# First blocks right behind their own group's turns, modulation weights in four slots, level products one slot later, four loads per chunk in the attention sweep

## What is computed

```python
mod = c_act @ w_mod[l] + b_mod[l]
shift, scale, gate = jnp.split(mod[:, None, :], 3, axis=-1)
h = rms_norm(x, g_pre[l]) * (1.0 + scale) + shift
(gq, gk, gv, ga_f, ga_b, gz, cq, ckv, kr, mz) = _split(h @ w_in_e[e], EVEN_SPLITS)

def step(state, inp):                      # GLA, one direction, one chunk
    qc, kc, vc, gc = inp
    b = jnp.cumsum(gc, axis=2)
    diff = b[:, :, :, None, :] - b[:, :, None, :, :]
    decay = jnp.exp(jnp.where(mask[None, None, :, :, None], diff, -jnp.inf))
    att = jnp.einsum('bhid,bhjd,bhijd->bhij', qc, kc, decay)
    o = jnp.einsum('bhij,bhjv->bhiv', att, vc) + jnp.einsum('bhid,bhdv->bhiv', qc * jnp.exp(b), state)
    b_last = b[:, :, -1, :]
    state = jnp.exp(b_last)[..., None] * state + jnp.einsum(
        'bhjd,bhjv->bhdv', kc * jnp.exp(b_last[:, :, None, :] - b), vc)
    return state, o
o = rms_norm((o_f + o_b).astype(z.dtype), g_norm).reshape(B, S, GLA_WIDTH)
return o * jax.nn.silu(z)
```

## Time and profile before

| | us |
|---|---|
| median of three runs | 3487.02 |
| lowest and highest | 3482.92, 3491.3 |
| profiled execution, its own time | 3487.6 |
| its span on the core | 3485.7 |
| PE busy (share of the span) | 3094.9 (89%) |
| DVE busy | 1376.7 (39%) |
| ACT busy | 1145.9 (33%) |
| POOL busy | 641.5 (18%) |

### The profile page before, as it was taken

The page is one execution under the profiler, slowest core; times in us unless marked ns, Lnnn a source line. Parts: engine busy times, 40 slices in busy tenths (PEclk is TensorE's granted clock), DMA queues, the critical chain, the costliest instruction groups (busy, mean ns, idle before and its releaser), DMA issues.

```text
span 3485.7 us, 47947 instructions
## 1 busy us (share of the span) xinstructions
PE 3094.9 (89%) x17396; PEld 2611.6 (75%) x17396; DVE 1376.7 (39%) x2428; ACT 1145.9 (33%) x2055; POOL 641.5 (18%) x565
## 2 busy tenths in 40 slices
PE   1788999755588999999899499999999999999999
PEld 1556888645577888888788388877888888877887
DVE  4356677511155767676532511112222222222111
ACT  1462245311224555555422611113333223323110
POOL 1021121034231212122122000002112112213221
PEclk6898999866679999999999799999999999999999
DMA  6132355463322111121155211112122122124322
GB/s 206 46 105 97 98 153 161 135 180 104 87 59 74 56 47 54 49 58 51 56 175 181 112 73 72 48 65 78 54 72 72 59 68 72 66 84 152 109 96 72
DMA packets 272009, 318.45 MB, mean 91 GB/s; under 512 B 26323, under 2 KB 206803, under 8 KB 268404
## 3 DMA queue, kind: packets, MB, share of 16 engines
q1 hardware_dynamic: 271894, 316.90, 28.1%
HBM read 214.07 MB, written 102.76 MB: 91 GB/s over the span
## 4 chain that ended last, share of the span: by engine, by line
PE 79%; issue 5%; DVE 4%; POOL 3%; DMA 3%; ACT 3%; SPq 1%; POOLq 0%; DVEq 0%; ACTq 0%
PE PS L325 11%; PE PS L326 10%; PE PS L327 10%; PE PS L2090 4%; PE PS L2091 4%; PE PS L2092 4%; PE PS L2195 3%; PE PS L2197 3%; PE PS L2196 3%; PE PS L1551 3%; PE PS L1573 2%; PE PS L1574 2%; PE PS L1575 2%; PE PS L1540 2%; PE PS L2333 2%
## 5 line engine op out<-in xcount | busy, mean ns | idle before, releaser
L325 PE MATMUL PS<-hTh,whi 128*128 128x512 f32 x1664 | 658.0, 395 | 7.5 <-POOL wlo L319 7.5
L326 PE MATMUL PS<-hTl,whi 128*128 128x512 f32 x1664 | 650.1, 391 | 0.0
L327 PE MATMUL PS<-hTh,wlo 128*128 128x512 f32 x1664 | 649.7, 390 | 0.0
L325 PEld LDWEIGHTS PS<-hTh,whi 128*128 128x128 f32 x1664 | 313.9, 189 | 80.6 <-issue 10.5
L327 PEld LDWEIGHTS PS<-hTh,wlo 128*128 128x128 f32 x1664 | 313.7, 189 | 66.2
L326 PEld LDWEIGHTS PS<-hTl,whi 128*128 128x128 f32 x1664 | 313.9, 189 | 62.8
L317 POOL TENSOR_TENSOR whi<-wraw,zero 128x1024 fp32r<-128x1024 f32 x52 | 99.9, 1922 | 1029.5 <-PE PS L327 975.5
L2090 PE MATMUL PS<-ow_h,of_h 128*128 128x512 f32 x576 | 225.0, 391 | 7.7 <-DVE oy L2047 7.7
L2091 PE MATMUL PS<-ow_l,of_h 128*128 128x512 f32 x576 | 224.8, 390 | 0.0
L2092 PE MATMUL PS<-ow_h,of_l 128*128 128x512 f32 x576 | 224.7, 390 | 0.0
L1649 ACT ACTIVATE pth<-PS 128x512 fp32r<-128x512 f32 x256 | 153.6, 600 | 188.9 <-PE PS L1551 188.9
(11 more groups left out here) (251 smaller groups left out, 6024.3 us busy)
## 6 DMA issues: line engine op xcount, KB each, us to landing
projT<-pev SPq DMA_DIRECT2D x80, 256.0 KB, 2.5
xt<-x SPq DMA_DIRECT2D x8, 2048.0 KB, 8.8
mw<-wmod SPq DMA_DIRECT2D x64, 256.0 KB, 2.8
oxt<-x SPq DMA_DIRECT2D x32, 512.0 KB, 4.8
sg_v<-vev SPq DMA_DIRECT2D x64, 256.0 KB, 2.3
wraw<-wuz SPq DMA_DIRECT2D x32, 512.0 KB, 5.7
vm<-sg_v SPq DMA_DIRECT2D x16, 1024.0 KB, 5.6
sgT<-mT SPq DMA_DIRECT2D x16, 1024.0 KB, 4.4
```

The source lines that it names most:

```text
L325: pe.matmul(PS[:, bank, :], w[1][:, s, k, :], hTh[:, k, b], start=(k == 0), stop=False)
L326: pe.matmul(PS[:, bank, :], w[1][:, s, k, :], hTl[:, k, b], start=False, stop=False)
L327: mm = pe.matmul(PS[:, bank, :], w[2][:, s, k, :], hTh[:, k, b], start=False, stop=(k == KD - 1))
```

## The change

- **Modulation weights.** `mw0` has four slots; load n waits for sum n-4. The first eight tiles are those of the first half of the columns (shift), the next eight those of the second (scale), and PE makes the columns of a half when its eight sums are done. x of group 1 is loaded right behind the last modulation weights, and the first projection weights wait for all sums, since the slots now lie over `wraw0`.
- **First blocks.** Block 0 stands right behind turns 6 and 7; six turns of the next group follow block 0, 2 and 4, two follow blocks 1, 3 and 5. ACT's list follows.
- **Levels.** Each slot y now holds distances and exponential for y, products for y-1, PE's level products for y-1 and sums for y-2; loads run three units ahead. k and q have semaphores of their own, so that distances don't wait for them. The attention matrix is written to memory in the layout in which the sweep reads it, by two instructions of 64 partitions in place of one of 128, on DVE and on ACT.
- **The sweep.** Four loads a chunk (decays; k and q; values and states, now one tensor `gla_vs`; attention) and one for the gate input z, which has its own semaphore and is waited for only by the gate product. Load t+4 stands ahead of store t-2 in SP's list and waits for outputs t. Factors are made one round ahead. Contribution and outputs use other PSUM banks.

The diff, cut:

```diff
-        mw0 = at("mw0", X0 + 8 * K, [P, 2, D])
+        mw0 = at("mw0", X0 + 8 * K, [P, 4, D])
...
-        def mod_load(sp, k):
-            for j in range(2):
-                n = 2 * k + j
-                if n >= 2:
-                    sp.wait_ge(s_macc, n - 1)
-                sp.dma_start(mw0[:, j, :], a["wmod"][0, k * P:(k + 1) * P, j * D:(j + 1) * D]).then_inc(s_mw[j], 16)
+        def mod_load(sp, n):
+            half, k = n // KD, n % KD
+            if n >= 4:
+                sp.wait_ge(s_macc, n - 3)
+            sp.dma_start(mw0[:, n % 4, :], a["wmod"][0, k * P:(k + 1) * P, half * D:(half + 1) * D]).then_inc(s_mw[n % 4], 16)
...
-            mod_cols(pe, macc0, 0).then_inc(s_mps, 1)
+            for half in range(2):
+                pe.wait_ge(s_macc, KD * (half + 1))
+                mm = mod_cols(pe, macc0, half)
+            mm.then_inc(s_mps, 1)
...
-            for k in range(KD):
-                mod_load(sp, k)
+            for n in range(2 * KD):
+                mod_load(sp, n)
+            norm_load(sp, 0, (1,))
+            sp.wait_ge(s_macc, 2 * KD)
             for g in range(2):
                 proj_load(sp, g)
-            norm_load(sp, 0, (1, 2))
+            norm_load(sp, 0, (2,))
             for g in range(2, 4):
...
-                for half in range(2):
-                    for k in range(4):
-                        norm_act(act, 8 * g + 4 * half + k)
-                    proj_evict(act, 2 * g - 2 + half)
+                proj_evict(act, 2 * g - 2)
+                for k in range(6):
+                    norm_act(act, 8 * g + k)
+                proj_evict(act, 2 * g - 1)
+                for k in range(6, 8):
...
-            for m in range(6, 14):
+            for m in range(6, 8):
                 norm_pe(pe, m)
             for j in range(8):
                 proj_block(pe, j)
-                for m in range(12 + 4 * j if j else 14, min(16 + 4 * j, 32)):
-                    norm_pe(pe, m)
+                g = j // 2 + 1
+                if g < 4:
+                    for k in (range(6, 8) if j % 2 else range(6)):
+                        norm_pe(pe, 8 * g + k)
 
...
-            dve.wait_ge(s_ll[s], 48 * (t // 2 + 1))
+            dve.wait_ge(s_ll[s], 32 * (t // 2 + 1))
...
+            dve.wait_ge(s_lk[t % 2 * 2 + p], 16 * (t // 2 + 1))
...
-            dve.tensor_tensor(l_att[:, p, :, 0, :], x[:, :, 0:HB], x[:, :, 2 * HB:3 * HB], ALU.add).then_inc(s_ma, 1)
+            for b in range(2):
+                mine = slice(HB * b, HB * b + HB)
+                dve.tensor_tensor(l_att[mine, p, :, mine], x[mine, :, 0:HB], x[mine, :, 2 * HB:3 * HB], ALU.add).then_inc(s_ma, 1)
...
-            level_exp(act, 0)
             for y in range(NU):
                 j, n = 16 + 2 * y, y - Y_BACK
                 proj_evict(act, j)
-                if y + 1 < NU:
-                    level_exp(act, y + 1)
+                level_exp(act, y)
                 if n >= 0:
...
-            level_distances(dve, 0)
             for y in range(NU):
                 n = y - Y_BACK
                 if n >= 1:
                     back_state(dve, n - 1)
-                if y + 1 < NU:
-                    level_distances(dve, y + 1)
-                level_products(dve, y)
+                level_distances(dve, y)
+                if y:
+                    level_products(dve, y - 1)
                 if n >= 0:
                     back_turned(dve, n)
-                if y:
-                    level_sums(dve, y - 1)
+                if y >= 2:
+                    level_sums(dve, y - 2)
                 if n == -2:
...
-                level_pe(pe, y)
+                if y:
+                    level_pe(pe, y - 1)
+            level_pe(pe, NU - 1)
...
+                sp.dma_start(m_fe[:, s].rearrange("p d h c -> p (d h) c"), cumT[0:4, :, tok].rearrange("n p c -> p n c")
+                             ).then_inc(s_ml[s], 16)
+                sp.dma_start(m_kq[:, s].rearrange("p h w c -> p (h w) c"), projT[T_GK:T_GK + 4, :, tok].rearrange("n p c -> p n c")
+                             ).then_inc(s_ml[s], 16)
+                sp.dma_start(m_vs[:, s, :], gla_vs[t, :, :]).then_inc(s_ml[s], 16)
+                sp.wait_ge(s_las[0], 16 * (t + 1))
+                sp.wait_ge(s_las[1], 16 * (t + 1))
+                sp.dma_start(attT[:, s, :, :], gla_a[t, :, :, :]).then_inc(s_ml[s], 16)
+
+            def load_z(t):
+                if t >= 4:
                     sp.wait_ge(s_mgz, t - 3)
-                for dst, src in ((m_f, cumT[0:2, :, tok]), (m_e, cumT[2:4, :, tok])):
-                    sp.dma_start(dst[:, s, :, :], src.rearrange("h p c -> p h c")).then_inc(s_ml[s], 16)
-                for w, r in ((0, T_GQ), (1, T_GK)):
-                    sp.dma_start(m_qk[:, s, w, :, :], projT[r:r + 4:2, :, tok].rearrange("h p c -> p h c")).then_inc(s_ml[s], 16)
-                sp.dma_start(m_v[:, s, :], gla_v[t, :, :]).then_inc(s_ml[s], 16)
-                sp.dma_start(attT[0:HB, s, :, :].rearrange("p h c -> p (h c)"),
-                             gla_a[t, 0:HB, :, :, :].rearrange("p h d c -> p (h d c)")).then_inc(s_ml[s], 16)
-                for d in range(2):
-                    sp.dma_start(attT[HB:P, s, :, HB * (1 - d):HB * (2 - d)], gla_a[t, HB:P, :, d, :]).then_inc(s_ml[s], 16)
-                sp.dma_start(m_s[:, s, :, :].rearrange("p h v -> p (h v)"), gla_sb[t, :, :]).then_inc(s_ml[s], 16)
-                sp.dma_start(m_z[:, s, :, :], projT[T_GZ:T_GZ + 4, :, tok].rearrange("h p c -> p h c")).then_inc(s_ml[s], 16)
+                sp.dma_start(m_z[:, t % 4, :, :], projT[T_GZ:T_GZ + 4, :, t * P:(t + 1) * P].rearrange("h p c -> p h c")
+                             ).then_inc(s_mzl[t % 4], 16)
 
             def store(t):
                 sp.wait_ge(s_mgz, t + 1)
                 sp.dma_start(mixT[0:GH, :, t * P:(t + 1) * P].rearrange("h p c -> p h c"), og[:, t % 2, :, :]
                              ).then_inc(s_mst[t % 2], 16)
             sp.wait_ge(s_pb, 8 + NBLK)
-            for j in (NBLK - 2, NBLK - 1):
-                stored(sp, j)
             sp.wait_ge(s_bvs, 16 * NT)
             for u in range(2):
                 sp.wait_ge(s_bss[u], 8 * NT)
-                sp.wait_ge(s_las[u], 16 * NT)
             for t in range(4):
                 load(t)
+            for j in (NBLK - 2, NBLK - 1):
+                stored(sp, j)
+            for t in range(4):
+                load_z(t)
+            for u in range(2):
+                sp.wait_ge(s_las[u], 16 * NT)
             rot_sp(sp)
             latents_sp(sp)
-            for t in range(NT):
-                store(t)
+            for t in range(NT + 2):
                 if t + 4 < NT:
                     load(t + 4)
+                if t >= 2:
+                    store(t - 2)
+                    if t + 2 < NT:
+                        load_z(t + 2)
...
             factors(0)
-            factors(1)
...
-                if t + 2 < NT:
-                    factors(t + 2)
+                if t + 1 < NT:
+                    factors(t + 1)
...
+                pool.wait_ge(s_mzl[t % 4], E_mzl + 16 * (t // 4 + 1))
...
-            pe.wait_ge(s_mm, NU)
-            pe.wait_ge(s_mb, NU)
+            pe.wait_ge(s_mm, NU - 1)
+            pe.wait_ge(s_mb, NU - 1)
+            pe.wait_ge(s_pev, NBLK)
```

More of the change, by code:

```diff
@@ L140, in emit @@
         s_gp = sem("s_gp")
-        s_mw = [sem("s_mw0"), sem("s_mw1")]
+        s_mw = [sem("s_mw%d" % j) for j in range(4)]
         s_mz = sem("s_mz")
@@ L396, in start_dve @@
             norm_dve_front(dve, 0)
-            for k in range(KD):
-                mod_sum(dve, k)
+            for n in range(2 * KD):
+                mod_sum(dve, n)
             mod_end(dve, 0)
@@ L654, in level_across @@
                 act.wait_ge(s_las[p], 16 * t)
-            act.activation(l_att[:, p, :, 1, :], PS[:, 2 + 2 * p:4 + 2 * p, NLV * HB:4 * P], ACT.Copy).then_inc(s_mb, 1)
+            for b in range(2):
+                mine = slice(HB * b, HB * b + HB)
+                op = act.activation(l_att[mine, p, :, HB * (1 - b):HB * (2 - b)], PS[mine, 2 + 2 * p:4 + 2 * p, NLV * HB:4 * P],
+                                    ACT.Copy)
+            op.then_inc(s_mb, 1)
         kt = at("kt", X0 + 60 * K, [P, 2, P])
@@ L777, in proj_sp @@
             gates_store(sp, NG - 1)
-            for t in range(2):
-                for p in range(2):
-                    level_fe(sp, t, p)
+            proj_load(sp, 6)
+            for tp in ((0, 0), (0, 1)):
+                level_fe(sp, *tp)
             level_kq(sp, 0, 0)
+            level_fe(sp, 1, 0)
             for y in range(NU):
-                t, p, j, n = y // 2, y % 2, 16 + 2 * y, y - Y_BACK
-                if p == 0 and j // 4 + 2 < N_TILES:
+                j, n = 16 + 2 * y, y - Y_BACK
+                if y and y % 2 == 0 and j // 4 + 2 < N_TILES:
                     proj_load(sp, j // 4 + 2)
@@ L829, in proj_act @@
                     back_factors(act, 0)
-                if y:
```

(15 more changed lines are left out.)

106 lines of the change are left out of this document (52 added, 54 removed).

## The result

The changed kernel takes 3330.24 us, the median of four runs (3325.59 to 3336.38), against 3486.34 for the kernel before in four runs beside it (3482.92 to 3491.3). The ratio is 0.9552, 95% interval 0.9533 to 0.9572. The forecast was 3338, range 3312 to 3374. The profiled execution of the changed kernel took 3336.38 us for a span of 3334.6, so it was the slowest of the four. Against the profiled execution before (3487.6) it gives 151.2, where 150 was forecast; the medians give 156.1. Of PE's idle time before, the first 1200 us held 299 of 391 us, which is three quarters and not nearly all; the change works on that part.

What follows compares the result with a forecast made beforehand. PE, 79% of the chain of waits, was taken as the bound, with gains in four stretches where it has no work: 32 + 15.8 + 11 + 91 = 150 us, so 3487.6 - 150 = 3338 us, range 3312 to 3374.

Steps and rivals of the forecast that it cites:

- (a): Start, modulation sums and first eight projection blocks: four weight slots and reordered blocks gain 32 us (20 to 37).
- three cycles of a group: Start: block, squares to turns, turns, block, turns and h, about 20.5 to 21 us each, 62.5 for three.
- Rival 3: Start: four weight slots do not help, a load costs 2.5 us; 13.6 us more, 3351; chance 0.12.
- (b): Start of the levels: products one slot later let blocks 18 and 19 run first; gain 15.8 us (10 to 19).
- (c): Sweep's head, last level store to first contribution: less store waiting and fewer loads; gain 11 us (8 to 12).
- (d): Sweep: loads issued before the store hide their latency, 248.0 us becomes 157; gain 91 us (68 to 107).
- the restart behind them: Sweep: a term of 9.8 us to restart behind chunk 4.
- Rival 2: Sweep: no exclusion between POOL's pass and DVE's q product; POOL's 8.32 us sets the round; 3326; chance 0.12.
- Rival 1: Sweep: PE's clock stays low, rounds take 10.9 us, 131 in place of 108; 3361; chance 0.18.
- Rival 4: Sweep: stays bound by its loads as SP waits in order; 97 us more, 3435; chance 0.06.
- Rival 5: Levels: every slot stretches, outweighing the gain from 4.7 us a slot, so slower than before; chance 0.02.
- The signs named beforehand: Whole kernel: expected trace signs, including splits near 140 us, PE idle under 1 us before level products, one sweep load wait.

## Why the prediction was right, point by point

- **(a) Start, gain 32:** measured 32.0, with errors that cancel. A sum took 1.59 us ((46.83 + 1.28 - 22.60)/16), not 1.38, so the columns ended at 51.7 and not 47.9: sums that had their weights came 1.39 us apart, but 4.0 us of waits stayed. The slices from 26 to 52 us show 333 GB/s on average, not 421. The three cycles of a group took 60.1 us (first block of each group at 67.75, 86.96, 106.59 and 127.87) and not 62.5. The terms written for a cycle add up to 21.8 us, not to the 20.5 to 21 that were used. In the earlier trace rows the slices from 24.5 to 59.5 us read 70 to 293 GB/s, 204 on average, not 150 to 260. For the sums the estimate of 1.46 us by the Trainium skill (DMA: Bandwidth & Descriptors, "Where 436 GB/s comes from") was nearer than my 1.38; yet slices with a full queue reach 415 to 429 GB/s in this trace too, so a limit of 358 is not what holds the sums; a slot that is loaded again only behind its sum fits both runs: behind the weights loaded ahead, a sum comes every 1.70 us with four slots and every 2.70 with two, that is, 6.8 and 5.4 us for a slot from one sum to its next. Rival 3 is refuted by the run with two slots.
- **(b) Levels, gain 15.8:** measured 17.8 on PE (last block 676.12 to 626.3, less the start's 32.0) and 3.1 lost at the end, 14.7. The sum was right, its cause half wrong: by the run with the products in their own slot over half of it is there without the shift, and the semaphore of k and q is what the rows show for it. The block that the prediction let start near 263.6 did so (231.87 + 32.0 = 263.9).
- **(c) Head, gain 11:** 8.7 (19.9 to 11.2). The step that failed is the landing: 5.46 us and not 2.9. Sixteen loads are issued within some 11 us there; that they share the queues is the likely cause, and no run tested it.
- **(d) Sweep, gain 91:** measured 98.9. Chunk 4's factors came 34.7 us behind the first contribution (forecast 36) and the restart behind them took 3.3 us, not 9.8, a term for which the prediction shows no row. The rounds sum up to 107.9, as forecast (108), but the sorts are different. Rounds with a 5.4 us pass take 8.4 to 8.5, not 10.2: that pass does not shut DVE out to its end. Rounds with a 4.5 us two-input pass take 9.0 (forecast 9.3). The other rounds behind chunk 4 take 8.0 to 9.8, not 7.4, at a granted clock of 0.50 to 0.78; at 1.00 such a round takes 7.4 (8.0 with the 3.6 us pass), in this kernel ahead of chunk 4 (655.51 to 662.90) and in the one with moved loads. The same four rounds take 30.2 us there and 35.9 here, so 5.7 us go with the low clock, where the forecast had 4 in a term of its own. Four rounds 1.8 shorter than forecast, and against them the four 1.6 longer (less the 4 us for the clock, which are in them) and one round more (5.5) came out even, and this was luck.
- **Rival 2** is right for one-input passes and wrong for two-input ones. **Rival 1** was half seen: the clock is 0.66 to 0.70 in the rounds with a 5.4 us pass from 709 us on, but costs nothing where POOL sets the round (8.4 us at 1.00 and at 0.66). Where PE does, it costs 0.4 and 2.3 us in the two rounds behind chunk 4 and 0.6 and 2.4 in the two behind the last long pass, not 23 in all. **Rival 4** fell, though the price of 97 was near (66 + 22 + 14 = 103). **Rival 5**: the slots kept their 12.2 us.
- The signs named beforehand were there, save four: the columns' end (51.7, not 46 to 50), the first contribution (55.3 us sooner, not 59), the two lengths of rounds (8.4 and 9.0, not 7 to 8 and 9 to 10.5) and the granted clock, 0.80 over the sweep but under 0.8 in seven of its rounds. One sum still waited over 1 us (1.1).
- The range's lower end, 3312, needs 107 for (d); with the 100 written beside it the terms give 3320. The result lies inside either.

## What to carry to other kernels

Before costing an in-order queue, draw the ring: store, load, the first use, and then each engine's own order back to the next store; here a product for the next chunk ahead of the mean on DVE, and that mean's power ahead of the gate on POOL, closed a ring in which the early load was worth 66 us, while six issues fewer were worth 14. Large transfers that nobody needs soon go in pieces behind the loads that somebody waits for (16.5 us here). Before work goes from POOL to DVE, ask which short operation of POOL will run beside it: a pass that nobody waits for can still hold up one that is waited for.

## What was unexpected on the hardware

- **Exclusion depends on the form.** Beside a two-input pass of POOL (4.52 us, to 725.06) DVE's q product stood still: two that take 1.40 us took 2.54 and ended 1.3 behind the pass. Beside a one-input pass (5.38 us, to 709.17) the same two took 2.22, 0.8 longer than alone, and ended while the pass still ran. In the other direction both of DVE's forms held POOL to their end. The Trainium skill (SBUF — State Buffer, "SBUF: two separate sides") says that the port pair shared by DVE and POOL is "an exclusive lock", and that the later of the two "fully blocks". The traces agree for the two pairs with a two-input pass. They do not for POOL's one-input pass, and for DVE's one-input pass they agree on the block but not on the order: POOL's power, which was held, starts at 694.17 by its row, ahead of the pass at 694.64.
- **POOL's pass with one operation is slower than with two.** Of the 128x2048 passes those with a scalar operation alone took 5.37 to 5.38 us, those with two 1.90; on DVE both took 1.22. Whether a second, empty operation would save 3.5 us in each of four rounds was not tried.
- **The clock fell behind some gaps of 2 us on PE, not behind all.** The window from 709.15 has 0.70, a mix of 1.2 and 2.4 GHz, around the gap of the row below; the one ahead of it has 1.00. With the latent loads moved, the window from 692.69 to 701.18 kept 1.00 around a gap just as long (2.05 us), and the next, with 2.13, had 0.67. With eight matmuls in that place no window from 650 to 770 us fell below 1.00. What decides between the two cases stays open.

```profile
710.93 0.44 PE L1115 MATMUL PS<-ident,m_kf 128*128 128x128 f32 x2 [2.05 <-POOL m_kf L1081]
```
